# Two chained transformer blocks on one core: a part of the values stage moved into the second layer's sum of experts' results

## The reference, cut to what matters

```python
for li in range(2):                                   # first block, two layers, 1040 tokens (16 + 1024), width 1024
    ...                                               # attention and recurrence, w_out, layer norm
    ff = _hier_moe(h, ...)                            # 32 experts, two of them for each token
    h = _layer_norm(DN_ALPHA * h + ff, ln2_g[li], ln2_b[li])
x = h[:, 16:]                                         # 1024 tokens go on
# second block
proj = jnp.einsum('bsd,de->bse', x, w_in_2[0])        # 1024 x 1024 by 1024 x 2560
va = proj[..., 1024:1536]                             # the values of the attention   (first value product)
u, vg = proj[..., 1536:2048], proj[..., 2048:2560]    # for the spatial gating        (third and second product)
```

## Time and profile before

| | us |
|---|---|
| three timed runs | 5394.4, 5400.27 (median), 5401.44 |
| the profiled execution, its own time | 5393.46 |
| its span in the profile | 5391.6 |
| the second layer's sum, first load issued to last low part | 3978.3 to 4077.7 |
| values stage, first weights issued to the second product's first block | 4078.4 to 4129.8 |

### The profile page before, as it was taken

The page is one execution under the profiler, slowest core; times in us unless marked ns, Lnnn a source line. Parts: engine busy times, 40 slices in busy tenths (PEclk is TensorE's granted clock), DMA queues, the critical chain, the costliest instruction groups (busy, mean ns, idle before and its releaser), DMA issues. The chain is left out here.

```text
span 5391.6 us, 128874 instructions
## 1 busy us (share of the span) xinstructions
PE 4819.5 (89%) x56564; PEld 4154.7 (77%) x56564; DVE 3312.1 (61%) x5055; ACT 2134.1 (40%) x3885; POOL 1304.3 (24%) x940
## 2 busy tenths in 40 slices
PE   6989999998799957989999997799957988999999
PEld 5888888886588847878888886588845766788887
DVE  5435665557788864345665557788875465662662
ACT  2323333332188842433333332188843244232331
POOL 0012333332144510012333332144411100122221
PEclk9999999998799977989999998799978989999999
DMA  4420101003366653410101004366652101233332
GB/s 135 140 53 19 32 20 31 19 19 114 119 229 254 251 174 97 124 53 20 31 20 31 19 19 115 120 231 251 251 172 86 39 1 67 90 98 121 110 98 106
DMA packets 383087, 536.31 MB, mean 99 GB/s; under 512 B 136483, under 2 KB 306595, under 8 KB 354467
## 3 DMA queue, kind: packets, MB, share of 16 engines
q1 hardware_dynamic: 339714, 488.61, 28.3%
q0 software_dynamic: 41472, 34.21, 2.1%
q10 hardware_dynamic: 1344, 5.24, 0.3%
HBM read 573.01 MB, written 122.09 MB: 129 GB/s over the span
## 5 line engine op out<-in xcount | busy, mean ns | idle before, releaser
L280 PE MATMUL ps<-w_hi,xbT 128*128 128x512 f32 x1536 | 502.3, 398 | 18.0 <-DVE w L2437 18.0
L280 PE MATMUL ps<-hT,w_in 128*128 128x416 f32 (+1 forms) x2736 | 490.7, 338 | 9.0 <-DVE w_in L761 9.0
L280 PEld LDWEIGHTS ps<-hT,w_in 128*128 128x128 f32 x2736 | 457.3, 195 | 35.3 <-issue 29.3
L2437 DVE TENSOR_TENSOR w<-w,w_hi 128x2048 fp32r<-128x2048 f32 x192 | 429.9, 2278 | 2.2 <-ACT w_hi L2394 2.2
L1486 POOL TENSOR_TENSOR lm<-Ab,consts 116x416 f32<-116x416 f32 x240 | 254.8, 1069 | 592.0 <-PE ps L280 316.4
L2394 ACT ACTIVATE w_hi<-w 128x2048 fp32r<-128x2048 f32 x192 | 359.0, 1935 | 0.0
L280 PEld LDWEIGHTS ps<-w_hi,xbT 128*128 128x128 f32 x1536 | 289.6, 189 | 86.3 <-DVE w L2437 27.1
L280 PE MATMUL ps<-w,xbT 128*128 128x512 f32 x768 | 300.6, 391 | 0.0
L280 PE MATMUL ps<-v,pT 104*104 104x128 f32 (+1 forms) x2176 | 270.3, 280 | 28.2 <-issue 27.4
L2468 DVE TENSOR_TENSOR w<-w,w_hi 128x2048 fp32r<-128x2048 f32 x96 | 223.5, 2328 | 97.0 <-ACT w_hi L2430 97.0
L280 PEld LDWEIGHTS ps<-v,pT 104*104 104x104 f32 (+1 forms) x2176 | 248.8, 178 | 39.9 <-issue 32.4
(11 more groups left out here) (449 smaller groups left out, 11384.9 us busy)
## 6 DMA issues: line engine op xcount, KB each, us to landing
w<-in_moe_w_dram SPq DMA_DIRECT2D x192, 1024.0 KB, 10.0
w_gate<-in_w_gate_dram SPq DMA_DIRECT2D x44, 512.0 KB, 3.9
w_up<-in_w_up_dram SPq DMA_DIRECT2D x44, 512.0 KB, 3.9
w_down<-in_w_down_dram SPq DMA_DIRECT2D x44, 512.0 KB, 3.2
w_in<-in_w_in_dram SPq DMA_DIRECT2D x36, 512.0 KB, 4.3
ys<-t_ys SPq DMA_DIRECT2D x20, 832.0 KB
t_h<-x SPq DMA_DIRECT2D x30, 416.0 KB
w_out<-in_w_out_dram SPq DMA_DIRECT2D x24, 512.0 KB, 7.3
```

The lines of the kernel that those rows point to most:

```text
L280: made = e.matmul(out, a, b, start=start, stop=stop)
L2437: e.tensor_tensor(w.lo, w.x, w.hf, ALU.subtract).then_inc(*P.c("moe_dve").tick(li, "w13", b, k))
```

## The change

The first value product is taken apart. Its weights (and the second product's) are loaded in rounds 0 to 7 of the second layer's sum, two pieces a round; ScalarE makes the first product's high parts in rounds 1 to 4 and the second's in rounds 6 to 9; GpSimd makes all eight low parts of the first product, and the second's are made after the sum as before. TensorE runs blocks 0 to 6 of the first product behind the transposes of tiles 2, 3, 4, 6, 7, 8 and 9 (`AFTER`), each once the low part of the tile before is there, and ScalarE copies block n out at the end of round `AFTER[n] + 3`. Block 7 and the transposes of the spatial matrices stay behind the sum.

To make room, both layers' sums get three `ys` buffers instead of four and three pairs of PSUM banks instead of four (banks 0 and 3 take the product's blocks); `ys` of tile r+2 is loaded in round r once tile r-1's weighted sum is done, ahead of the store of tile r-2 in SyncE's order, and `h` of tile r+1 after that store as before. `ys` of tile 3 is no longer loaded before the rounds.

```diff
-SHARED.update({f"com_{s}_in": f"sp_w{8 + s}_in" for s in range(4)})
+SHARED.update({f"com_h{s}_in": f"moe_w3{s}_in" for s in range(4)})
+SHARED.update({f"com_y{s}_in": f"moe_w2{s}_in" for s in range(3)})
...
+NY = 3
+AFTER = (2, 3, 4, 6, 7, 8, 9)
...
+def turn_bank(P, i, half):
+    return P.ps[((1, 2), (4, 5), (6, 7))[i % 3][half]]
...
 def combine_sp(e, P, li):
-    def load(i):
-        s = i % NS
-        if i >= NS:
-            e.wait_ge(*P.c("com_pe").at(li, i - NS, 1))
-            e.wait_ge(*P.d(f"com_h{s}_out").at(li, i - NS))
-        e.dma_start(m.yv[s][0:C], T["ys"][...]).then_inc(...)
-        e.dma_start(m.hx[s][0:C, :], T["h"][C * i:C * i + C, :]).then_inc(...)
-    load(0)
-    load(1)
+    def load_sum(i):
+        if i >= NY:
+            e.wait_ge(*P.c("com_dve").at(li, i - NY, "y", 1))
+        e.dma_start(m.yv[i % NY][0:C], T["ys"][...]).then_inc(*P.d(f"com_y{i % NY}_in").tick(li, i))
+    def load_rest(i):
+        s = i % NS
+        if i >= NS:
+            e.wait_ge(*P.c("com_pe").at(li, i - NS, 1))
+            e.wait_ge(*P.d(f"com_h{s}_out").at(li, i - NS))
+        e.dma_start(m.hx[s][0:C, :], T["h"][C * i:C * i + C, :]).then_inc(*P.d(f"com_h{s}_in").tick(li, i))
+    for i in range(2):
+        load_sum(i)
+        load_rest(i)
     ...                                                    # gain and bias
-    load(2)
-    load(3)
+    load_sum(2)
+    load_rest(2)
+    load_rest(3)
     if li == 0:
         project_first(e, P, 1)
-    for t in aged(NT, 4):
+    for r, t in enumerate(aged(NT, 4)):
+        if li and r < 8:
+            for k in range(2 * (r % 4), 2 * (r % 4) + 2):
+                values_load(e, P, r // 4, k)
+        if t[1] is not None and t[1] + NY < NT:
+            load_sum(t[1] + NY)
         ...                                                # the store of h, tile t[2]
         if t[3] is not None and t[3] + NS < NT:
-            load(t[3] + NS)
+            load_rest(t[3] + NS)
...
 def combine_act(e, P, li):                                 # at the end of a round
+        if li and 1 <= r < 5:
+            for k in range(2 * r - 2, 2 * r):
+                values_hi(e, P, 0, k)
+        if li and 6 <= r < 10:
+            for k in range(2 * r - 12, 2 * r - 10):
+                values_hi(e, P, 1, k)
+        if li and r - 3 in AFTER:
+            values_first_out(e, P, AFTER.index(r - 3))
...
 def combine_dve(e, P, li):                                 # before the weighted sum
+            e.wait_ge(*P.d(f"com_y{i % NY}_in").at(li, i))
...
 def combine_pe(e, P, li):                                  # behind the transposes of tile i
+        if li and i in AFTER:
+            n = AFTER.index(i)
+            e.wait_ge(*P.c("com_dve").at(li, i - 1, "lo", 1))
+            values_product(e, P, 0, n)
...
+def values_product(e, P, n, i):
+    out = P.ps[3 * (i % 2) + n][:, :]
+    if i >= 2:
+        e.wait_ge(*ac.at(0, "ev", n, i - 2))
+    for k in range(8):
+        if i == 0:
+            e.wait_ge(*P.c("val_pool" if k % 2 or n == 0 else "val_dve").at(0, "lo", n, k))
+        made = mms(e, three(out, P.xT2.at(k, slice(128 * i, 128 * i + 128)), m.w[n % 2].at(k), k == 0, k == 7))
+    made.then_inc(*P.c("val_pe").tick(0, "mm", n, i))
+def values_early_pool(e, P):                               # on GpSimd between MOE and COMBINE of the second layer
+    for k in range(8):
+        values_lo(e, P, 0, k, P.c("val_pool"))
...
 def values_sp(e, P):
-    weights(0)
     ...                                                    # spatial matrices, bias, gain
-    weights(1)
     e.wait_ge(*P.c("val_pe").at(0, "mm", 0, 7))
-    weights(2)
+    for k in range(8):
+        values_load(e, P, 2, k)
...
 def values_act(e, P):
-    weights(0, range(8))
-    weights(1, range(8))
-    for i in range(8):
-        e.wait_ge(*pe.at(0, "mm", 0, i))
-        e.activation(P.vt2[:, i, :], P.ps[3 * (i % 2)][:, :], ACT.Copy).then_inc(*ac.tick(0, "ev", 0, i))
+    values_first_out(e, P, 7)
...
 def values_pe(e, P):
-    for i in range(8):
-        product(0, i)
-        if i == 1:
-            ...                                            # transposes of the spatial matrices
+    values_product(e, P, 0, 7)
+    ...                                                    # transposes of the spatial matrices
```

More of the change, by code:

```diff
@@ L2515 @@
     f"moe_{x}{k}{s}_in" for s in range(NL) for x in "wg" for k in (1, 2, 3)) + tuple(f"moe_x{s}_in" for s in range(NX))
+NY = 3
+AFTER = (2, 3, 4, 6, 7, 8, 9)
+VALUES_TOP = 47560
 def combine_mem(P):
[L2522 to L2527, removed]
+    P.com = []
+    for li in range(DEPTH):
+        P.top = P.after_router
+        m = Box()
+        m.yv = [P.region2(2, D, "ys") for _ in range(NY)]
+        m.tmp = [P.region(16, "stat") for _ in range(NS)]
+        m.hx = [P.region(D, "h")]
+        if li:
+            P.top = VALUES_TOP
+        m.gt, m.bt = P.region(D, "gain"), P.region(D, "bias")
+        m.hx += [P.region(D, "h") for _ in range(NS - 1)]
+        P.com.append(m)
 def combine_norm(P, li, i):
-    m = P.com
+    m = P.com[li]
     return Norm(P, (P.c("com_dve"), P.c("com_act")), (li, i), m.hx[i % NS], C, m.tmp[i % NS], m.gt, m.bt)
+def turn_bank(P, i, half):
+    return P.ps[((1, 2), (4, 5), (6, 7))[i % 3][half]]
 def combine_part(P, li, i, half):
@@ L2655, in values_mem @@
     m.w.append(P.split(8, 512, "wv"))
+    assert P.top == VALUES_TOP
     m.wsp, m.wT = P.region2(4, 128, "wsp"), P.region2(4, 128, "wspT")
@@ L2661, in values_mem, with values_load @@
     P.b2_top = P.top
+def values_load(e, P, n, k):
+    e.dma_start(P.val.w[n % 2].x[:, k, :], P.T["w_in_2"][0, 128 * k:128 * k + 128, VCOLS[n]:VCOLS[n] + 512]).then_inc(
+        *P.d(f"val_w{n % 2}{k}_in").tick(0, n))
 def values_sp(e, P):
     m, T, into = P.val, P.T, P.d("val_in")
[L2667 to L2670, removed]
-    weights(0)
     e.dma_start(m.wsp, T["w_spatial_2"][0].rearrange("g t s -> t g s")).then_inc(*into.tick(0, "w"))
@@ L2733, in values_act @@
         if 1 <= i < 5:
-            weights(2, range(2 * i - 2, 2 * i))
+            for k in range(2 * i - 2, 2 * i):
+                values_hi(e, P, 2, k)
     for i in range(8):
@@ L2788, in values_pe @@
     m, pe, dv, ac = P.val, P.c("val_pe"), P.c("val_dve"), P.c("val_act")
-    def product(n, i):
-        out = P.ps[3 * (i % 2) + n][:, :]
-        if i >= 2:
-            e.wait_ge(*ac.at(0, "ev", n, i - 2))
-        for k in range(8):
-            if i == 0:
-                e.wait_ge(*(P.c("val_pool") if k % 2 else dv).at(0, "lo", n, k))
-            made = mms(e, three(out, P.xT2.at(k, slice(128 * i, 128 * i + 128)), m.w[n % 2].at(k), k == 0, k == 7))
-        made.then_inc(*pe.tick(0, "mm", n, i))
     def mix(i):
@@ L2807, in mix @@
         mms(e, [(pg[:, g, :], m.wT[:, g, :], z3[:, g, :], True, True) for g in range(4)]).then_inc(*pe.tick(0, "mix", i))
+    values_product(e, P, 0, 7)
+    pv = groups4(P.ps[7][:, :])
+    e.wait_ge(*P.d("val_in").end(0))
+    trs(e, P, [(pv[:, g, :], m.wsp[:, g, :]) for g in range(4)]).then_inc(*pe.tick(0, "wT"))
     for i in range(8):
-        product(0, i)
-        if i == 1:
-            pv = groups4(P.ps[7][:, :])
-            e.wait_ge(*P.d("val_in").end(0))
-            trs(e, P, [(pv[:, g, :], m.wsp[:, g, :]) for g in range(4)]).then_inc(*pe.tick(0, "wT"))
-    for i in range(8):
-        product(1, i)
+        values_product(e, P, 1, i)
         if i >= 2:
@@ L2819, in values_pe @@
     for i in range(8):
-        product(2, i)
+        values_product(e, P, 2, i)
         if i < 2:
@@ L3759, in gpsimd_program @@
         over(e, P, li, *MOE)
+    values_early_pool(e, P)
     over(e, P, 1, *COMBINE)
```

52 lines of the change are left out of this document (26 added, 26 removed).

## The result

The kernel after takes 5372.28 us (median of five, 5368.55 to 5376.3) against 5400.27 (median of five beside them, 5394.4 to 5407.66): ratio 0.9948, 95% interval 0.9934 to 0.9963. The forecast was 5369. In the profiled executions the span went from 5391.6 to 5366.7 us, 24.9 less.

What follows compares the result with a forecast made beforehand. VectorE was taken to bound the second layer's sum, the DMA queue close behind, TensorE with room. -39.5 + 8.9 + 2.7 = -27.9 us from a base of 5397.3 gave 5369 us, range 5354 to 5386.

Steps and rivals of the forecast that it cites:

- What bounds: Second layer's sum: VectorE bounds at 8.52 us a round, DMA queue close behind; TensorE works 1.65 us and has room.
- One sign: Second layer's sum: the new profile would show granted clock near 1.00 for most rounds.
- What is taken off the end, -39.5: From tile 9's weighted sum to the second product: 63.5 us becomes 24.0, a gain of 39.5 us.
- The DMA queue, +8.9: Second layer's sum: added weights make h(4) late, tile 4's weighted sum +6.6 us, tile 9's 8.9 late; bounds 0 and 12.
- the queue's sum: Transfer prices added up in SyncE's one queue, in order: h(4) lands at 4029.1, 50.9 us after the first load.
- Port and ScalarE's order: Before tile 4's weighted sum: GpSimd low parts up to 1.0 us each, ScalarE's wait 3.3; some 7 us, covered by h(4)'s wait.
- none of the eight goes free: Rounds 1 to 4: every GpSimd low part excludes VectorE, unless VectorE reads PSUM just then; up to 1.0 us each.
- The first layer, +2.7: First layer's sum: three result buffers for four make h(4) late, tile 4's weighted sum +2.7 us; bounds 0 and 6.
- (1): Second layer's sum: transfers fit, h(4) comes in time and the sum keeps its rounds; 5358 to 5361 us; chance 0.2.
- (2): Second layer's sum: port and ScalarE's order cost on top, +8 to +14 us; 5377 to 5383 us; chance 0.15.
- (3): Second layer's sum: TensorE's clock stays at the lower level, 12.6 us a round; 5406 us; chance 0.05.
- (4): Second layer's sum: block 0 waits for late weights and holds tile 3's transposes, some 15 us; 5384 us; chance 0.05.

Runs made afterwards that it cites:

- e4: Kernel after, with all eight blocks of the first product and their copies kept behind the sum, weights still loaded and split inside it: 5407.61 us.
- e9: e3 with ScalarE's high parts of the first product moved to rounds 2 to 4: 5366.36 us, one run.
- e6: Kernel after, with idle matmuls behind the transposes of tiles 3 to 9 to fill TensorE's pauses: 5374.09 us.
- e10: Kernel after, unchanged, run again on the same chip as e11: 5368.79 us.
- e5: Kernel after, with the first layer's sum given back its four result buffers and old load order: 5371.94 us.
- e2: Kernel after, with the sixteen weight loads inside the sum bringing 32 of 512 columns each: 5374.82 us.
- e1: Kernel after, with GpSimd filling the eight early low parts with zeros (only writing) instead of subtracting: 5371.93 us.
- e3: Kernel after, with the edits of e1 and e2 together (zero-filled low parts, small weight loads): 5369.71 us.
- e7: Kernel after, with SyncE in each round storing h, then loading h, results and weights, in both layers: 5365.57 us.
- e11: e8 unchanged, run again beside the kernel after on one chip: 5366.36 us.
- e8: Kernel after, with SyncE's order of e7 and ScalarE's first-product high parts in rounds 2 to 4: 5365.37 us.

## Why the prediction was right, point by point

**What bounds.** TensorE had room in the sum: e4 and e9 show that the blocks cost it nothing, and e4 that they are the whole gain. One sign was not met: the granted clock was not near 1.00 in most rounds (0.79 and 0.67 in the stretches above), and the blocks fitted into their rounds all the same.

**What is taken off the end, -39.5.** Measured -38.0. The gap is the clock at block 5, 7.33 us where I used 5.44. In the runs where it took 5.75 the stretch is 29.45 us: 68.98 - 29.45 = 39.5, the forecast. I had taken (7% idle, clock 1.00) for enough; that stretch stands for a TensorE that rests 7% of the time, and in the sum it rests some 2 us of a round of 8.52 behind a block at the higher clock. Blocks 0 and 3 started low as said (8.39 and 7.44 us), inside the round's room; that blocks 2 and 5 would fall was not in the prediction. Its 5.44 us a block was low as well: its own rows give 49.26 / 9 = 5.47, and a single block at the higher clock took 5.7 to 5.8. To the second product itself it was 25.3 us for the 24.0 of the sum.

**The DMA queue, +8.9.** Measured +8.3 for the whole sum in this profile, and +8.6, +10.2 and +11.9 in the other three (e6, e10, e5). h(4) landed 51.4 us after the first load where the queue's sum had 50.9. The landing was right; that it is the cause of 8.3 us is half the truth. Port and ScalarE's order, which I priced at some 7 us "at the same place" and let the queue cover, do cost that much by themselves (e2: 7.1), and the queue with ScalarE's order does too (e1: 9.8). At tile 4's sum the two lanes (the queue on one side, the port on the other, each with ScalarE's order) are nearly level: 52.9 us without the port, 51.4 without the weights' bytes, 52.5 with both. The queue, which I named, is the longer one by about a microsecond at most, which one execution of each can't make sure. The Trainium skill's 13 engines for 104 rows ("DMA: Bandwidth & Descriptors", the section on why a DMA increments its semaphore by 16) fit here as well: no rescue came from the idle ones, and h(4) landed where the full price of the weights puts it. Up to tile 4 it was +7.1 where I had +6.6. Behind it I had +2.3 for the queue alone; it was +1.1 here and +1.5 to +3.8 in the other three, and 0.9 to 1.0 us of it is the port's hold on tile 4's weighted sum (e2, without the weights' bytes, has +1.0; e3, without either, 0.0). So the size was about right, and the cause again shared.

**The port.** Up to 1.0 us for each low part: tile 2's sum lost 1.9 for two, tiles 3 and 4 1.0 and 0.9, besides a gain-and-bias step of 2.09 for 1.28. Together that is 3.9 us before tile 4's sum, where I had six low parts at 1.0, and 0.9 in it. The 0.77 us of room a round that I took off was not used: VectorE still waits 0.77 us for ScalarE's copy. With the 2.8 us that it lost between tiles 1 and 2 this makes 6.7, so the "some 7 us" came out right by two errors that cancel. Nor did every low part that met VectorE hold it: the two statistics operations at 4016.84 and 4017.45, beside a subtraction, took their 0.69 and 0.68 us, so "none of the eight goes free" was too strong. The rule of the Trainium skill ("SBUF — State Buffer", "Who interferes with whom") holds in both halves here: the subtractions held VectorE, the fill that reads no SBUF did not (e1).

**The first layer, +2.7.** +3.7 in this profile and +3.0 as the mean of eight. Counted from the first load, SyncE came free 3.9 us sooner (I had 4), results 3 were 1.85 us late where I had them in time, and h(4) was the last wait, as said. In the total it can't be found.

**The rivals.** (1) failed: h(4) came 51.4 us after the first load, and e1 shows VectorE waiting for it. (2) was right that the port costs, though 4.8 us and not eight times 1.0, and wrong that it comes on top. (3) failed, but for the 1.6 us that a block at the lower clock costs at the end. (4) failed: block 0 was through at 4038.8 (4030.43 + 8.39) and tile 3's transposes right behind it, before ScalarE wanted them in its next round (4046.97).

**The base.** 5393.5 for the profiled execution and 5400.3 for the median left 7 us of choice. The gain of the medians is 28.0, the sum had 27.9. That they agree to 0.1 is luck: the interval of the ratio leaves 20 to 36 us, and in the two profiles the three terms came to -38.0 + 8.3 + 3.7 = -26.0. The +1.1 of "all else" doesn't mean that nothing else moved: it is +2.8 before the first sum, -4.1 between the sums and +2.4 behind the second product's first GELU.

## What to carry to other kernels

Work put beside a stage costs what the fullest of its lanes can't take, and two lanes that are late in the same rounds hide each other: take one away alone and little moves, which proves nothing about either. Price each lane to the same instruction (here tile 4's weighted sum) and take the largest; then, to gain, mend all of them. In a queue served in order, put what is waited for next (the store that frees a buffer, the load behind it) ahead of what is needed rounds later.

## What was not expected of the hardware

Pauses of nearly the same length had different outcomes. Ahead of block 5 TensorE stood 1.66 to 1.94 us in e1, e2, e3 and e7, and the block took 5.74 to 5.78; it stood 2.06 to 2.09 us in the kernel after, its repeat, e5, e9 and e11, and the block took 7.31 to 7.37; but in e8 it stood 2.07 and the block took 5.75. Other blocks cross over further: block 2 took 5.78 behind 2.06 us in e7 and 5.74 behind 2.59 us in e5, and 7.30 behind 2.68 us in e1; block 1 took 7.36 behind 2.06 us in e2 and 5.75 behind 2.59 us in e1. So the length of the pause ahead of a block does not tell which it will be, and what does stays open. In the kernel after, the clock fell not in the pause but some 0.3 us into block 5. And GpSimd's fills of 128 x 512 took 1.05 us for two beside VectorE at full speed, where two subtractions of that size took 3.61 and 4.08 us while a weighted sum of 2.60 took 3.50 to 3.60.
